# Hybrid decoder block with mixture of experts: down weights in 16 KB rows, column tiles on pairs of activation columns

## The chip, the cores and the metric

The kernel runs on one core of a Trainium2 chip. The metric is device time in microseconds, the median of three executions. A core has TensorE (PE, matmuls, with a weight load called PEld that can overlap them), VectorE (DVE), ScalarE (ACT), GpSimd (POOL) and SyncE (SP). All weights lie in HBM and are brought to SBUF, 128 partitions of on-chip memory, by 16 DMA engines; SP issues nearly all transfers here. TensorE writes its results to PSUM.

## What is computed

One decoder layer: a mixer (an S5 state-space branch beside a convolution branch), then a mixture of 32 experts of which each of 256 tokens takes 4. The mixer ends before the part that this document is about. Of the reference, the experts:

```python
for e in range(N_EXPERTS):                       # 32
    gu = hf @ w_gate_up[e] + b_gate_up[e]        # (256, 1024) @ (1024, 2048)
    g, lin = gu[:, :D_EXPERT], gu[:, D_EXPERT:]
    g = jnp.minimum(g, SWIGLU_LIMIT)
    lin = jnp.clip(lin, -SWIGLU_LIMIT, SWIGLU_LIMIT)
    act = g * jax.nn.sigmoid(SWIGLU_ALPHA * g) * (lin + 1.0)
    out = out + combine[:, e:e + 1] * (act @ w_down[e] + b_down[e])   # (256, 1024) @ (1024, 1024)
```

Everything is fp32. An expert has 8 MiB of gate_up weights and 4 MiB of down weights.

## The kernel before

About the first 230 us belong to the mixer and to the router. Then the experts run in **blocks** of 32 token slots: an expert has at least one block, and more if more than 32 tokens chose it. The number of blocks is read at run time from a plan that VectorE makes; with these inputs there are 46. TensorE runs one block after the other.

**Tiling of a block.** With 32 tokens only 32 columns of the TensorE array would be used, so four matmuls run side by side in four column tiles q = 0 to 3 (`NQ`, `BS` = 32 slots, `QW` = 256 columns). Column tile q works on 256 of the 1024 expert columns and writes PSUM partitions 32q to 32q+31. `bias` (L1450) first writes the gate_up bias into PSUM bank 0, 4 matmuls of 512 columns. `gate_up` (L1461) adds 8 contraction steps k of 4 matmuls; each has 32 tokens as stationary operand (`xT`) and 2 x 256 weight columns as moving operand: 256 for g and 256 for lin, read as two runs of neighbouring words, `row[:, :, QW * q:QW * q + QW]`. An fp32 matmul is two instructions in the trace, so a block's gate_up is 64. `after_gate_up` then scatters the block before, gathers the next tokens (L1418, L1427), transposes the activation in two matmuls (L1489, which read every second column j = 0, 1) and runs `down` (L1474) in two halves h, with `selection` (L1443) and the transpose of the next tokens (L1436) between them.

**Which column is where.** Because L1489 takes every second column, partition p of the transposed activation holds columns 256q + 2p + j. The rows of the down weights must be in the same order: `dn_rows` gives partition p the rows 256q + 2p and 256q + 2p + 1, for the two q of a half. Two rows of 4 KB are 8 KB of neighbouring bytes, and a half has two such runs per partition.

**Loads.** SP issues them in order. Each expert is six DMAs of 2 MiB: four of gate_up (`load_gu`, L365, per partition 16 KB of neighbouring bytes) and two of down (`load_dn`, L368). There are buffers for two experts, `gsl[e % 2]` and `dsl[e % 2]`, so a load for expert e waits until the last block of expert e - 2 has read that buffer (`gu_done`, `dn_done`, with `used_by` from the plan). Of the last expert, the second down half comes in two DMAs (L473, L474). The bias of gate_up comes in four small DMAs (L431) into `bias_rows`, partitions 32q to 32q+31 holding the 32 experts' 2 x 256 columns of tile q.

Of the kernel before, what the change touches and what calls it, by code (L numbers as in the profile page):

```python
# [29 lines left out]
P = 128  # L30
D = 1024
# [12 lines left out]
EXP = 32  # L44
TOPK = 4
BS = 32
NQ = P // BS
QW = D // NQ
# [7 lines left out]
SLOT = 2048  # L56
# [16 lines left out]
def build(nc, T, out):  # L73
    with ExitStack() as ctx:
        def sb(name, shape, dt=F32):
            return ctx.enter_context(nc.sbuf_tensor(name, shape, dt))

        def sem(name):
            return ctx.enter_context(nc.semaphore(name))
# [12 lines left out]
        rC, rD, rE = (ring, C_AT), (ring, D_AT), (ring, E_AT)  # L92
# [3 lines left out]
        rU, rQ = (late, 0), (late, MT * L)  # L96
        rT, rP = (late, 2 * MT * L), (late, 2 * MT * L + 1024)
        rW = sb("rW", [P, 1024])
        base = sb("base", [P, 344 + 3 * 256])
        rX1, rX2, rX3 = (base, 344), (base, 344 + 256), (base, 344 + 512)  # L100

        def view(r, at, *dims, rows=P, dt=F32):
            n = 1
            for d in dims:
                n *= d
            words = n // 2 if dt == BF16 else n
            if isinstance(r, tuple):
                r, at = r[0], r[1] + at
            v = r[0:rows, at:at + words]
            if dt != F32:  # L110
                v = v.bitcast(dt)
            if len(dims) == 2:
                v = v.rearrange("p (a b) -> p a b", b=dims[1])
            if len(dims) == 3:
                v = v.rearrange("p (a b c) -> p a b c", b=dims[1], c=dims[2])
            if len(dims) == 4:
                v = v.rearrange("p (a b c d) -> p a b c d", b=dims[1], c=dims[2], d=dims[3])
            return v
# [49 lines left out]
        rw = view(rF, D, KT, EXP)  # L168
        rb = view(rF, D + 256, EXP)
        hf = [view(rE, 640, D), view(rW, 0, D)]  # L170
        bias_rows = view(rE, 1664, 2 * QW)
        squares = view(rW, 0, D)
        squares2 = view(rC, 2048, 2 * ST, 2, QW)
        scaled = view(ring, KT * SLOT + 2048, ST, NQ, QW)
# [1 line left out]
        xT = view(rX1, 0, 2, NQ, BS)  # L176
# [27 lines left out]
        ebias = view(base, 151, BS)  # L204
# [27 lines left out]
        ps = ctx.enter_context(nc.psum_tensor("ps", [P, 8, 512], F32))  # L232
# [10 lines left out]
        dn_in = [[sem(f"dn_{name}{n}") for n in range(2)] for name in ("even", "odd")]  # L243
# [33 lines left out]
        scales, dn_tail = sem("scales"), sem("dn_tail")  # L277
# [55 lines left out]
        dsl = [[view(ring, DN_AT + odd * DN_ODD + h * 4096, 4096) for h in range(2)] for odd in range(2)]  # L333
# [5 lines left out]

        def dn_rows(e, h):  # L340

            return T["w_down"][0, e].rearrange("(q p j) n -> p q (j n)", q=NQ, j=2)[:, 2 * h:2 * h + 2, :]

        def out_cols(q):

# [5 lines left out]
        def _(sp):  # L351
# [13 lines left out]
                sp.dma_start(gsl[e % 2][n], gu_rows(e, n)).then_inc(gu_in[e % 2][n], 16)  # L365

            def load_dn(e, h):
                sp.dma_start(dsl[e % 2][h].rearrange("p (q c) -> p q c", q=2), dn_rows(e, h)).then_inc(dn_in[e % 2][h], 16)  # L368

            for n in range(2):  # L370
                load(n)
# [12 lines left out]
            for a in range(TG):  # L384
                h = min(SH, TAPS - SH * a)
# [43 lines left out]
            sp.dma_start(gffn, T["norm_ffn_g"][0:1, :].to_broadcast([P, D])).then_inc(late_in, 16)  # L429
            for q in range(NQ):  # L430
                sp.dma_start(bias_rows[BS * q:BS * q + EXP, :].rearrange("e (a c) -> e a c", a=2),  # L431
                             T["b_gate_up"][0].rearrange("e (a n) -> e a n", a=2)[:, :, QW * q:QW * q + QW]
                             ).then_inc(bgu_in, 16)
            used_up(sp, N_IN + 3)
            load_gu(0, 1)
# [18 lines left out]
            def used_by(e):  # L454

                return sp.value_load(blk_last[0:1, e:e + 1], min_val=0, max_val=NBLK - 1)

            for e in range(2, EXP):
                before = used_by(e - 2)
                for n in range(NPAIR):  # L460
                    sp.wait_ge(gu_done, before * KT + PAIR * (n + 1))
                    load_gu(e, n)
                if e < EXP - 1:
                    for h in range(2):
                        sp.wait_ge(dn_done, before * KT + 4 * (h + 1))
                        load_dn(e, h)
                    whole(dn_tail)
                else:
                    sp.wait_ge(dn_done, before * KT + 4)
                    load_dn(e, 0)  # L470
                    sp.wait_ge(dn_done, before * KT + KT)
                    halves = dn_rows(e, 1)
                    sp.dma_start(dsl[e % 2][1][:, 0:SLOT], halves[:, 0, :]).then_inc(dn_in[e % 2][1], 16)  # L473
                    sp.dma_start(dsl[e % 2][1][:, SLOT:], halves[:, 1, :]).then_inc(dn_tail, 16)  # L474
            sp.wait_ge(dn_done, used_by(EXP - 2) * KT + KT)
            sp.dma_start(gfin, T["norm_final_g"].rearrange("(a n) -> a n", a=1).to_broadcast([P, D])
                         ).then_inc(fin_in, 16)
# [684 lines left out]
        def _(pe):  # L1162
# [3 lines left out]
            for c, rows, at in ((2, META, 0), (0, P, META), (1, P, META + P)):  # L1166
                pe.wait_ge(x_in[c], 16)
                for k in range(KT):
                    if c == 2 and k == KT - 1:
                        pe.wait_ge(gmix_cols, 1)  # L1170
                    ins = nc.tensor.transpose(ps[:, k, at:at + rows], xin[0:rows, c, k * P:(k + 1) * P],
                                              ident[0:rows, 0:rows])
# [159 lines left out]
            for n in range(KT):  # L1332
# [5 lines left out]
                for g in range(2):  # L1338
# [4 lines left out]
                    for k in range(MT):  # L1343
                        ins = nc.tensor.matmul(ps[:, bank(use), g * S:(g + 1) * S], w[:, k, (n % 4) * P:(n % 4) * P + P],  # L1344
                                               ya[:, k, :], start=(k == 0), stop=(k == MT - 1))
# [7 lines left out]
            for n in range(KT):  # L1353
# [5 lines left out]
                for k in range(MT):  # L1359
                    ins = nc.tensor.matmul(ps[:, bank(use), 0:S], w[:, k, (n % 4) * P:(n % 4) * P + P], cacc[:, k, :],  # L1360
                                           start=(k == 0), stop=(k == MT - 1))
# [23 lines left out]
            for c in range(ST):  # L1385
                for k in range(KT):
# [7 lines left out]
                    for h in range(2):  # L1394
                        ins = nc.tensor.matmul(ps[:, 4 + 2 * c + h, :], merged[:, k, c * P:(c + 1) * P],  # L1395
                                               w[:, k % 2, 512 * h:512 * h + 512], start=(k == 0), stop=(k == KT - 1))
# [50 lines left out]
            def bias():  # L1447

                for q in range(NQ):
                    nc.tensor.matmul(ps[BS * q:BS * q + BS, 0, :], ebias[BS * q:BS * q + EXP, :],  # L1450
                                     bias_rows[BS * q:BS * q + EXP, :], start=True, stop=False, skip_group_check=True,
                                     tile_position=(BS * q, BS * q))

            def gate_up(e, odd, first, until):
                for k in range(PAIR * first, PAIR * until):
                    n = k // PAIR
                    if k % PAIR == 0:
                        pe.wait_ge(gu_in[odd][n], e * 8 + 16 - 8 * odd)
                    row = gsl[odd][n][:, (k % PAIR) * SLOT:(k % PAIR) * SLOT + SLOT].rearrange("p (a c) -> p a c", a=2)
                    for q in range(NQ):  # L1460
                        ins = nc.tensor.matmul(ps[BS * q:BS * q + BS, 0, :].rearrange("p (a c) -> p a c", a=2),  # L1461
                                               xT[:, k % 2, k // 2, :], row[:, :, QW * q:QW * q + QW],
                                               start=False, stop=(k == KT - 1), skip_group_check=True,
                                               tile_position=(0, BS * q))
                    ins.then_inc(gu_done, 1)
# [53 lines left out]
            for c in range(ST):  # L1519
                ins = nc.tensor.matmul(ps[0:EXP, 1, 96:97], maskb[:, c, :], onesb[:, 0:1], start=(c == 0), stop=(c == 1))  # L1520
# [56 lines left out]
```

## Time and profile before

| | us |
|---|---|
| median of 3 executions | 1186.16 |
| lowest and highest | 1185.9, 1186.97 |
| the profiled execution | 1185.86 |
| its span in the trace | 1184.1 |
| TensorE busy in it | 982.7 (83%) |
| VectorE, ScalarE, GpSimd busy | 305.9, 143.0, 14.9 |

The page counts 69355 DMA packets with 435.39 MB. Of the chain that ended last, 43% of the span is TensorE and 41% DMA. How to read it: a busy TensorE is not one at its peak; a share over the whole span mixes stretches with different limits, so the stretches have to be looked at one by one. In a row of the trace the part behind "<-" is what was read, or what was waited for.

### The profile page before, as it was taken

Reading aid. Unit: us, or ns where it says so; the run is one execution under the profiler, and the core shown is the slowest. Engines: PE = TensorE matmul, PEld = TensorE weight load, DVE = VectorE, ACT = ScalarE, POOL = GpSimd, SP = SyncE. Lnnn points to the kernel's source line nnn. Section 1 sums busy time; section 2 is a strip of 40 time slices with the busy share of each in tenths; the row PEclk is TensorE's granted clock in tenths of the full one; section 3 lists DMA queues with packets and bytes.
Section 4 is the critical chain, followed back from the end, with each engine's and each line's share of the span. In section 5 each row is a group of like instructions: output and inputs, shape, how many; then the busy total and the mean of one; then the engine's idle time right before and its main releaser. Section 6 shows DMA issues by size and latency. Waiting matters only on the chain.

```text
span 1184.1 us, 23761 instructions
## 1 busy us (share of the span) xinstructions
PE 982.7 (83%) x10042; PEld 457.3 (39%) x10043; DVE 305.9 (26%) x908; ACT 143.0 (12%) x335; POOL 14.9 (1%) x26
## 2 busy tenths in 40 slices
PE   8999999979986666659999987689766898876685
PEld 6887886423332222223333332233222333322232
DVE  5999842511110000001111111011100111110012
ACT  2311230301110000001111110011000100100012
POOL 1111000000000000000000000000000000000000
PEclk9999999989998788899999999899988999998898
DMA  9772786791999999998899999999999999999994
GB/s 260 225 181 95 261 337 249 296 415 50 431 426 426 426 426 427 427 426 366 341 390 401 426 426 425 425 426 428 426 425 426 426 426 426 426 426 426 426 427 183
DMA packets 69355, 435.39 MB, mean 368 GB/s; under 512 B 15104, under 2 KB 31424, under 8 KB 36560
## 3 DMA queue, kind: packets, MB, share of 16 engines
q1 hardware_dynamic: 69184, 434.93, 89.7%
q8 instruction: 18, 0.29, 0.1%
q10 hardware_dynamic: 144, 0.09, 0.0%
q14 instruction: 9, 0.07, 0.0%
HBM read 432.21 MB, written 1.05 MB: 366 GB/s over the span
## 4 chain that ended last, share of the span: by engine, by line
PE 43%; DMA 41%; DVE 9%; SPq 3%; issue 2%; ACT 1%; ACTq 0%; DVEq 0%
DMA ring<-in_w_down 20%; PE ps L1461 16%; DMA ring<-in_w_gate_up 16%; PE ps L1474 8%; DMA early<-in_w_gate_up 4%; PE ps L1450 2%; PE ps L1344 2%; PE ps L1395 2%; PE ps L1206 2%; SPq L368 2%; PE ps L1427 2%; PE ps L1418 2%; SPq L365 1%; PE ps L1360 1%; PE ps L1443 1%
## 5 line engine op out<-in xcount | busy, mean ns | idle before, releaser
L1461 PE MATMUL ps<-ring,base 128*32 128x512 f32 x2208 | 283.3, 655 | 81.0 <-DMA ring<-in_w_gate_up 80.9
L1474 PE MATMUL ps<-ring,base 128*32 128x256 f32 x2944 | 177.9, 382 | 41.0 <-DMA ring<-in_w_down 22.6
L1461 PEld LDWEIGHTS ps<-ring,base 128*32 128x32 f32 x2208 | 67.3, 115 | 290.0 <-issue 162.4
L1474 PEld LDWEIGHTS ps<-ring,base 128*32 128x32 f32 x2944 | 90.2, 110 | 100.3 <-ACT base L693 31.4
L1123 DVE TENSOR_SCALAR base<-ps 128x256 f32<-128x256 f32 x46 | 19.5, 425 | 390.1 <-PE ps L1461 390.1
L1206 PE MATMUL ps<-ring 128*128 128x256 f32 (+1 forms) x448 | 102.5, 387 | 0.0
L1130 DVE COPY base<-ps 128x256 f32<-128x256 f32 x46 | 19.5, 425 | 312.3 <-PE ps L1474 312.3
L691 ACT ACTIVATE base<-base 128x256 f32<-128x256 f32 x46 | 19.2, 416 | 661.9 <-DVE base L1123 661.9
L1206 PEld LDWEIGHTS ps<-ring 128*128 128x128 f32 x448 | 84.4, 191 | 15.1 <-issue 1.4
L1450 PE MATMUL ps<-ring,base 32*32 32x512 f32 x368 | 51.4, 628 | 24.1 <-issue 23.6
L1461 PE MATMUL ps<-early,base 128*32 128x512 f32 x368 | 50.6, 673 | 17.8 <-DMA early<-in_w_gate_up 17.7
L1461 PE MATMUL ps<-late,base 128*32 128x512 f32 x368 | 47.0, 630 | 16.5 <-DMA late<-in_w_gate_up 16.5
L1427 PE MATMUL ps<-base,late 32*128 32x256 f32 x752 | 58.1, 426 | 2.2 <-issue 2.2
L1427 PEld LDWEIGHTS ps<-base,late 32*128 32x128 f32 x752 | 36.8, 201 | 51.0 <-issue 49.2
L1108 DVE TENSOR_SCALAR early<-base 128x32 f32<-128x32 f32 x92 | 23.4, 298 | 39.1 <-issue 36.5
L1461 PEld LDWEIGHTS ps<-early,base 128*32 128x32 f32 x368 | 11.7, 117 | 52.2 <-DMA early<-in_w_gate_up 27.2
L1418 PE MATMUL ps<-ring,early 128*32 128x256 f32 x376 | 30.2, 392 | 1.1 <-DVE early L1064 1.1
L1461 PEld LDWEIGHTS ps<-late,base 128*32 128x32 f32 x368 | 11.4, 112 | 48.3 <-DMA late<-in_w_gate_up 24.2
L1443 PE MATMUL ps<-base,early 128*32 128x128 f32 x736 | 29.6, 279 | 0.0
L677 ACT COPY base<-ps 128x256 f32<-128x256 f32 x47 | 17.5, 372 | 100.0 <-PE ps L1436 100.0
L1418 PE MATMUL ps<-rW,early 128*32 128x256 f32 x376 | 28.9, 379 | 0.0
L1344 PE MATMUL ps<-late,ring 128*128 128x256 f32 x128 | 28.2, 380 | 0.5 <-issue 0.5
(328 smaller groups left out, 682.7 us busy)
## 6 DMA issues: line engine op xcount, KB each, us to landing
ring<-in_w_gate_up SPq DMA_DIRECT2D x96, 2048.0 KB, 38.1
ring<-in_w_down SPq DMA_DIRECT2D x63, 2048.0 KB, 40.6
late<-in_w_gate_up SPq DMA_DIRECT2D x16, 2048.0 KB, 40.5
early<-in_w_gate_up SPq DMA_DIRECT2D x16, 2048.0 KB, 39.8
ring<-in_w_in SPq DMA_DIRECT2D x14, 1024.0 KB, 7.8
ring<-in_w_out SPq DMA_DIRECT2D x4, 1024.0 KB, 12.5
ring<-in_w_s_lin SPq DMA_DIRECT2D x2, 1024.0 KB, 6.3
ring<-in_w_s_gate SPq DMA_DIRECT2D x2, 1024.0 KB, 5.1
```

What stands on the lines that cost most here:

```text
L368: sp.dma_start(dsl[e % 2][h].rearrange("p (q c) -> p q c", q=2), dn_rows(e, h)).then_inc(dn_in[e % 2][h], 16)
L1108: ins = nc.vector.tensor_scalar(wsel[:, c, :], slots, cur[:, c:c + 1], cur[:, 2 + c:3 + c], ALU.is_equal, ALU.mult)
L1123: nc.vector.tensor_scalar(act_in, g_out, LIMIT, None, ALU.min).then_inc(g1_ready, 1)
L1206: ins = nc.tensor.matmul(ps[:, z % 2, 0:L - n0], w[:, k, (z % 2) * P:(z % 2) * P + P], h[:, k, n0:L], start=(k == 0), stop=(k == KT - 1))
L1344: ins = nc.tensor.matmul(ps[:, bank(use), g * S:(g + 1) * S], w[:, k, (n % 4) * P:(n % 4) * P + P], ya[:, k, :], start=(k == 0), stop=(k = ...
L1395: ins = nc.tensor.matmul(ps[:, 4 + 2 * c + h, :], merged[:, k, c * P:(c + 1) * P], w[:, k % 2, 512 * h:512 * h + 512], start=(k == 0), sto ...
L1418: ins = nc.tensor.matmul(ps[BS * q:BS * q + BS, 2, 0:QW], onehot[:, c, :], hf[c][:, QW * q:QW * q + QW], start=(c == 0), stop=(c == ST - 1 ...
L1427: ins = nc.tensor.matmul(ps[:, 4 + q, QW * c:QW * c + QW], selT[BS * q:BS * q + BS, c * P:(c + 1) * P], ysb[BS * q:BS * q + BS, :], start= ...
L1443: ins = nc.tensor.matmul(ps[BS * q:BS * q + BS, 3, S + c * P:S + (c + 1) * P], of[:, c, :], ident[:, :], start=True, stop=True, tile_posit ...
L1450: nc.tensor.matmul(ps[BS * q:BS * q + BS, 0, :], ebias[BS * q:BS * q + EXP, :], bias_rows[BS * q:BS * q + EXP, :], start=True, stop=False, ...
L1461: ins = nc.tensor.matmul(ps[BS * q:BS * q + BS, 0, :].rearrange("p (a c) -> p a c", a=2), xT[:, k % 2, k // 2, :], row[:, :, QW * q:QW * q ...
L1474: ins = nc.tensor.matmul(ps[BS * q:BS * q + BS, 1, 0:QW], actT[:, n % 2, n // 2, :], row[:, out_cols(q)], start=(n == 0), stop=(n == KT - ...
```

## The change

Partition p of the down weights now gets four neighbouring rows 4p to 4p+3 of a half (512 rows), which are 16 KB of neighbouring bytes, in one run. So the transposed activation must hold, in partition p, columns 512h + 4p + j' with j' = 0 to 3. The transposes stay as they were (every second column of a column tile), so column tile q now works on the columns 512(q // 2) + 4n + 2(q % 2) + (0, 1): pairs, at every fourth. `gate_up` reads its moving operand in that pattern out of the same weight rows, and writes PSUM in the same order of addresses as before. `bias` reads its operand in the same pattern (`act_cols`); for this each group of 32 partitions of `bias_rows` holds 2 x 512 columns in place of 2 x 256, loaded by the same four DMAs, now of 128 KB each, into a new region at the end of `base` (8 KB more per partition). To make room, the scratch for software DMAs is set to 1024 bytes.

```diff
@@ the region for the bias @@
-        base = sb("base", [P, 344 + 3 * 256])
+        base = sb("base", [P, 344 + 3 * 256 + 2 * D])
...
-        bias_rows = view(rE, 1664, 2 * QW)
+        bias_rows = view(base, 344 + 3 * 256, 2 * 2 * QW)
@@ the down weights' rows, and the columns of tile q @@
         def dn_rows(e, h):
-            return T["w_down"][0, e].rearrange("(q p j) n -> p q (j n)", q=NQ, j=2)[:, 2 * h:2 * h + 2, :]
+            return T["w_down"][0, e].rearrange("(h p j) n -> p h (j n)", h=2, j=4)[:, h, :]
+
+        def act_cols(row, q):
+            return row.rearrange("p (a n j) -> p a n j", a=2, j=4)[:, :, :, 2 * (q % 2):2 * (q % 2) + 2]
@@ loads @@
             def load_dn(e, h):
-                sp.dma_start(dsl[e % 2][h].rearrange("p (q c) -> p q c", q=2), dn_rows(e, h)).then_inc(dn_in[e % 2][h], 16)
+                sp.dma_start(dsl[e % 2][h], dn_rows(e, h)).then_inc(dn_in[e % 2][h], 16)
...
                 sp.dma_start(bias_rows[BS * q:BS * q + EXP, :].rearrange("e (a c) -> e a c", a=2),
-                             T["b_gate_up"][0].rearrange("e (a n) -> e a n", a=2)[:, :, QW * q:QW * q + QW]
+                             T["b_gate_up"][0].rearrange("e (a h n) -> e a h n", a=2, h=2)[:, :, q // 2, :]
                              ).then_inc(bgu_in, 16)
...
-                    sp.dma_start(dsl[e % 2][1][:, 0:SLOT], halves[:, 0, :]).then_inc(dn_in[e % 2][1], 16)
-                    sp.dma_start(dsl[e % 2][1][:, SLOT:], halves[:, 1, :]).then_inc(dn_tail, 16)
+                    sp.dma_start(dsl[e % 2][1][:, 0:SLOT], halves[:, 0:SLOT]).then_inc(dn_in[e % 2][1], 16)
+                    sp.dma_start(dsl[e % 2][1][:, SLOT:], halves[:, SLOT:]).then_inc(dn_tail, 16)
@@ TensorE @@
             def bias():
                 for q in range(NQ):
-                    nc.tensor.matmul(ps[BS * q:BS * q + BS, 0, :], ebias[BS * q:BS * q + EXP, :],
-                                     bias_rows[BS * q:BS * q + EXP, :], start=True, stop=False, skip_group_check=True,
+                    nc.tensor.matmul(ps[BS * q:BS * q + BS, 0, :].rearrange("p (a n j) -> p a n j", a=2, j=2),
+                                     ebias[BS * q:BS * q + EXP, :], act_cols(bias_rows[BS * q:BS * q + EXP, :], q), start=True, stop=False, skip_group_check=True,
                                      tile_position=(BS * q, BS * q))
...
                     for q in range(NQ):
-                        ins = nc.tensor.matmul(ps[BS * q:BS * q + BS, 0, :].rearrange("p (a c) -> p a c", a=2),
-                                               xT[:, k % 2, k // 2, :], row[:, :, QW * q:QW * q + QW],
+                        half = row[:, :, 2 * QW * (q // 2):2 * QW * (q // 2) + 2 * QW]
+                        ins = nc.tensor.matmul(ps[BS * q:BS * q + BS, 0, :].rearrange("p (a n j) -> p a n j", a=2, j=2),
+                                               xT[:, k % 2, k // 2, :], half.rearrange("p a (n j) -> p a n j", j=4)[
+                                                   :, :, :, 2 * (q % 2):2 * (q % 2) + 2],
                                                start=False, stop=(k == KT - 1), skip_group_check=True,
                                                tile_position=(0, BS * q))
...
-    nc = bacc.Bacc("TRN2", target_bir_lowering=False, num_devices=1)
+    nc = bacc.Bacc("TRN2", target_bir_lowering=False, num_devices=1, dynamic_dma_scratch_size=1024)
```

No instruction is added, taken away or moved on any engine; only operands change.

## Rows read from the trace of the kernel before

**Rows 1.** The page, 40 equal slices of the span: GB/s moved by the DMA engines.
```profile
GB/s 260 225 181 95 261 337 249 296 415 50 431 426 426 426 426 427 427 426 366 341 390 401 426 426 425 425 426 428 426 425 426 426 426 426 426 426 426 426 427 183
```

**Rows 2.** Windows: length, busy us of PE, PEld, DVE, ACT, POOL, PEclk, DMA share, GB/s.
```profile
324.00:530.00 206.00, 140.64 (x1440) 47.70 (x1432) 21.67 (x80) 14.46 (x40) 0.00 (x0) 0.88 1.01 426
560.00:656.00 96.00, 91.46 (x1144) 36.88 (x1140) 17.56 (x66) 10.85 (x30) 0.00 (x0) 1.00 0.88 369
656.00:1136.00 480.00, 383.75 (x4358) 143.05 (x4350) 67.30 (x253) 42.23 (x117) 0.00 (x0) 0.94 1.01 426
```

**Rows 3.** The chain in order of time: start us, us, what; three pieces of it.
```profile
253.87 1.93 PE ps L1450 x8
...
328.17 1.68 SPq L365
...
530.22 1.93 PE ps L1474 x32
...
533.41 7.00 PE ps L1461 x64
...
548.20 1.06 PE ps L1450 x8
549.26 7.00 PE ps L1461 x64
...
659.48 32.41 DMA ring<-in_w_down
...
1093.68 42.44 DMA ring<-in_w_down
```

**Rows 4.** L1461 on PE, whole span: duration ns min/median/max, first and last start us.
```profile
L1461 PE MATMUL ps<-ring,base x2208: 592/592/1062, 231.6 to 1159.0; 128*32 128x512 f32 x184
L1461 PE MATMUL ps<-late,base x368: 592/592/1061, 261.1 to 1160.7; 128*32 128x512 f32 x184
```

**Rows 5.** Windows with only w_down packets, only gate_up packets, and the same again.
```profile
373.00:380.00 7.00, 6.53 (x74) 2.62 (x70) 1.19 (x3) 1.06 (x3) 0.00 (x0) 0.81 1.02 424
384.00:398.00 14.00, 7.23 (x52) 1.48 (x52) 1.74 (x8) 0.00 (x0) 0.00 (x0) 0.81 1.01 428
402.50:409.50 7.00, 6.53 (x62) 2.61 (x58) 1.19 (x3) 1.06 (x3) 0.00 (x0) 0.73 1.02 424
413.50:427.50 14.00, 7.79 (x52) 1.54 (x52) 1.74 (x8) 0.00 (x0) 0.00 (x0) 0.85 1.01 428
```

**Rows 6.** DMA, three windows: 372:381 (w_down), 383:399 (gate_up), 371.9:401.4 (packets alone).
```profile
DMA packets 480, 3.80 MB, mean 422 GB/s; under 512 B 16, under 2 KB 16, under 8 KB 16
q1 hardware_dynamic: 480, 3.80, 101.3%
...
DMA packets 466, 6.85 MB, mean 428 GB/s; under 512 B 48, under 2 KB 48, under 8 KB 48
q1 hardware_dynamic: 466, 6.85, 100.5%
...
DMA packets 1119, 12.58 MB, mean 426 GB/s; under 512 B 96, under 2 KB 96, under 8 KB 96
```

**Rows 7.** SP's queue in order of time: start us, us, what.
```profile
291.33 2.06 SPq L365 DMA_DIRECT2D ring<-in_w_gate_up  x2
```

**Rows 8.** PEld at two lines: L1489 reads every second word, L1436 neighbouring words.
```profile
L1489 PEld LDWEIGHTS ps<-base x92: 194/208/221, 241.2 to 1165.2; 128*128 128x128 f32 x92
L1436 PEld LDWEIGHTS ps<-base x94: 137/140/143, 230.4 to 1168.0; 128*128 128x128 f32 x94
```

**Rows 9.** PEld in order of time: two loads of each of those lines.
```profile
298.43 0.31 PEld L1489 LDWEIGHTS ps<-base 128*128 128x128 f32 x2 [0.41 <-issue]
...
301.27 0.20 PEld L1436 LDWEIGHTS ps<-base 128*128 128x128 f32 x2 [0.41 <-issue]
```

**Rows 10.** SP's queue in order of time, at the bias loads.
```profile
165.90 2.54 SPq L431 DMA_DIRECT2D ring<-in_b_gate_up  x4
173.68 0.34 SPq L365 DMA_DIRECT2D ring<-in_w_gate_up  x1
```

## What I expect of the time

> **What bounds the kernel now.** Read the slices first. From the eleventh slice (296 us) on the DMA engines move about 426 GB/s in nearly every slice, with a dip between 530 and 650 us [rows 1]. The stretches say it sharper: 426 GB/s from 324 to 530 us, 369 GB/s from 560 to 656 us while TensorE is busy 91.46 of 96 us, then 426 GB/s up to 1136 us [rows 2]. The chain of waits changes hands in the same places [rows 3]. It is TensorE's from 253.87 to 328.17 us, the transfers' until a piece of `w_down` releases TensorE at 530.22, TensorE's until 659.48, the transfers' until `w_down` lands at 1136.12, and TensorE's from there to the end. So there are two kinds of stretch. Where an expert has one block of 32 tokens, streaming its 12 MiB of weights takes longer than its matmuls; where experts with several blocks follow each other, TensorE is late. The chain holds 5 blocks in the first TensorE stretch, 8 in the second, 2 in the last: 15 gate_up groups of 7.00 us [rows 3]. Over the span there are 2208 + 368 gate_up matmuls [rows 4] and 368 more whose weights lie in `early`: 2944, or 64 in each of 46 blocks.
>
> **Term 1: down weights in 16 KB rows.** Per DMA of 2 MiB the change halves the packets: 256 of 8 KB become 128 of 16 KB; over 16 engines that is 16 against 8 for each. The rows of the profile show both sizes, since gate_up already moves 16 KB rows. Windows that hold only `w_down` run at 424 and 424 GB/s, windows that hold only gate_up at 428 and 428 [rows 5]. 2.097 MB at 424 is 4.946 us, at 428 it is 4.900: 0.046 us saved per DMA, the low bound. The packets themselves give the high bound [rows 6]. In the 9 us of 8 KB rows, 464 packets (480 less 16 small ones) took 101.3% of 16 engines: 16 x 9 x 1.013 / 464 = 314 ns each. In the 16 us of 16 KB rows, 418 packets took 100.5%: 615.5 ns each. Two of the small ones are 13.3 ns longer than one large one; 8 such pairs are 0.106 us per DMA. I take 0.075, the middle, because window edges cut packets in the first and busy time overlaps a little (over 100%) in the second.
>
> How many such DMAs lie on the path? Only those served while the queue is never empty and the landing releases TensorE. From 291.33 us, when the fourth expert's weights are first asked for [rows 7], to the landing at 530.22 are 239 us; one expert takes 29.5 us (12.58 MB in that window) [rows 6], so 8.1 experts or 16 down DMAs. In the TensorE stretch until 656 us the saving is not worth anything: DMA has idle time there. From 656.8 to 1136.1 us are 16.2 experts or 32 DMAs. Sum 48 x 0.075 = 3.6 us, with bounds 48 x 0.046 = 2.2 and 48 x 0.106 = 5.1. The last expert's second half is still cut into two DMAs of 8 KB rows, and it lands after the piece at 1136 that sets the end: nothing. The first three experts' down weights load before 291 us, where no piece of the chain is a transfer (its one gap is 7.12 us of "issue", a wait for nothing that the profile shows): nothing.
>
> Here a rule of the Trainium skill is worth weighing. [rows 6] show 13.3 ns for an extra packet and the rates in [rows 5] 0.046 us over 8 packets, or 5.8 ns. The Trainium skill (DMA: Bandwidth & Descriptors, "Why small descriptors are slow (HBM only)") states a fixed cost of about 3 cycles per packet inside the DMA engine and calls joining descriptors worthwhile only up to 256 B; at the 850 MHz that page gives, 3.5 ns x 8 x 48 is an estimate of 1.4 us in place of 3.6, or 1184.8.
>
> **Term 2: gate_up reads its moving operand in pairs.** The count of matmuls, their shapes and the order stay. Each still streams 512 columns, but now 2 of every 4 neighbouring fp32 words, while another column tile reads the other 2. This cost is not in the trace: no matmul before reads its moving operand with a step. Bounds from rows: at the low end nothing (not below: the same columns are streamed and no instruction is saved). At the high end stands the only strided read of TensorE, the weight load of the activation's transpose (every second word): 208 ns against 140 for the same load of neighbouring words [rows 8], a factor 1.49. Which is nearer? Look at what that strided load delivers. Two of them fill 0.31 to 0.32 us, of which one is 0.208, so the second begins about 0.11 us after the first: 128 columns in 0.11 us, 0.86 ns each. Two contiguous ones fill 0.20 us, 0.06 us apart: 0.47 ns each [rows 9]. A gate_up group needs less than that contiguous rate: 64 matmuls, four side by side, in 7.00 us are 437 ns for 512 columns, 0.85 ns each. One strided stream with two useful words in 16 bytes thus delivers just what an fp32 matmul takes, and pairs also keep 8 bytes together. I take zero. What speaks against it is that four column tiles read at once, and four strided streams at once are not in the trace.
>
> The Trainium skill (Advanced Engine Details and Errata, "SBUF Cachelines") says that at least two hits in a 16-byte line give full performance. Pairs have two, so by that rule term 2 is zero and the sum stays. The weight load in [rows 8] also has two hits and is slower than the contiguous one: here the row does not agree, so I don't let the rule carry the zero.
>
> The `bias` matmuls read pairs too; 8 of them in 1.06 us, in every block [rows 3]; same reasoning, zero, or half of it at the factor 1.49. What covers a slower gate_up: only the one-block experts in the DMA stretches (TensorE is busy 140.64 of 206 us there [rows 2]). In the 15 blocks on the chain there is no cover.
>
> **Term 3: the rest.** The four bias loads double from 64 to 128 KB and are issued at 165.90 us [rows 10]. That is 0.25 MiB more, 0.6 us at 428 GB/s, and they wait for nobody's buffer: the next load on the same queue is issued 5 us later, at 173.68. They now land in a region of their own. Taken as zero; 0.6 us if the cover were gone. The smaller scratch for software DMAs touches no transfer of this kernel: all sit in queues of SP and ACT. PSUM is written in the same order as before, so nothing changes for VectorE and ScalarE; and the transposes read as before.
>
> **The sum** against the profiled run: 1185.86 measured, of which the span is 1184.1, so 1182.3 there. That run is 0.3 us under the median, so against 1186.16: 1186.16 - 3.6 = **1182.5 us**.
>
> **Rivals.** *A, the packets cost less than they seem, or other waits absorb it.* The rates are the only direct comparison and their low bound gives 2.2 us or less: 1184.0 to 1186.2. For it: 424 and 428 differ by 1%, near what such a window can resolve. Against it: two pairs of windows agree, and packet times point the same way. The estimate from the Trainium skill above, 1184.8, falls in this case.
>
> *B, four strided streams starve TensorE.* Place: gate_up and bias, 7.00 + 1.06 = 8.06 us per block. It decides from a slow-down of 3%: 15 blocks x 8.06 = 121 us, and 3.6/121 = 3%. At factor 1.49 a block gets 4 us longer. About 3.5 blocks lie before DMA restarts at 291 us (14 us), 8 in the middle (32), 2 at the end (8); less 3.6: 1186.2 + 50 = about 1236. At factor 2 a block would take 15.9 + 8.1 = 24 us (15.9 is from one start of gate_up to the next [rows 3]); two-block experts are then all slower than their weights, and TensorE's own floor decides: 253.9 + 45 x 24 + 12 after the last block = 1346. For it: the factor in [rows 8], and the doubling of the stored bytes that each stream walks over. Against it: the rate in [rows 9] suffices, and gate_up's matmuls take 592 ns as minimum and as median over the whole span, while DMA, VectorE and ScalarE use the same memory beside them [rows 4]: nothing there looks near a limit.
>
> *C, the change doesn't do what it says:* if the hardware cut 16 KB rows for `w_down` otherwise than for gate_up, the packets stay. Against it: gate_up's 128 x 4096 words give 16 KB packets [rows 6]. It ends as A.
>
> **Chances.** Forecast 0.60 (1181 to 1184), A and C 0.16 (1184 to 1187), B 0.24, of which mild (3 to 10%, up to 1195) 0.06, near 1.5 times 0.10, near 2 times 0.08. The range is 1180.5 to 1191: it takes in the forecast's bounds, A, and the mild end of B; the heavy B of 0.18 is left out. About 0.2% (2.4 us) is what a measurement of this kernel can tell from no change, so the line is at 1183.8: of the forecast's 0.60, 0.04 falls inside. Faster 0.56, same 0.21, slower 0.23.
>
> **What the profile after would show.** Right: `w_down` packets of 16 KB, some 8,000 packets fewer in all; about 428 GB/s in stretches that had 426; gate_up at 7.0 us for 64 matmuls, 592 ns median; `w_down` released TensorE about 1.2 us earlier at 530 and 3.6 us earlier at 1136. A: packets halved, rate at 426. B: gate_up groups over 7.2 us, and DMA idle in more slices. Wrong altogether: the 592 ns median moves, or the landing at 530 does not.

## The result, and the profile after

| | before | after |
|---|---|---|
| median of 20 runs each, us | 1185.38 | 1187.74 |
| lowest and highest, us | 1184.41, 1186.97 | 1185.64, 1188.79 |
| profiled execution, us | 1185.86 | 1186.65 |
| its span, us | 1184.1 | 1184.9 |

The changed kernel takes 1.0019 times the time of before, 95% interval 1.0012 to 1.0026: 2.4 us more, just inside the 0.2% that the prediction set as its line. The forecast was 1182.5. The time is within the range of 1180.5 to 1191, but it moved to the other side: 5.2 us above the forecast. The profiled execution of after lies 1.1 us under its median and that of before 0.5 us above its own, so the two traces differ by only 0.8 us of span.

The page of after: GB/s in 40 slices, and the packets of the whole run.
```profile
GB/s 257 228 189 89 269 346 239 307 408 45 432 427 430 428 429 429 427 429 349 345 381 382 430 428 428 429 426 431 427 429 426 429 428 428 429 428 429 427 428 163
DMA packets 61291, 435.65 MB, mean 368 GB/s; under 512 B 15104, under 2 KB 31168, under 8 KB 36560
```
The windows of after (columns as in [rows 2]).
```profile
324.00:530.00 206.00, 141.16 (x1468) 47.23 (x1464) 21.66 (x81) 14.46 (x40) 0.00 (x0) 0.91 1.01 428
560.00:656.00 96.00, 91.96 (x1110) 35.61 (x1106) 17.46 (x66) 10.20 (x28) 0.00 (x0) 1.00 0.86 361
656.00:1136.00 480.00, 388.34 (x4404) 142.54 (x4396) 67.34 (x254) 42.99 (x119) 0.00 (x0) 0.95 1.01 428
```
The transfers do what was foretold: 428 GB/s where [rows 1, 2] have 426. Only in the middle do they move less, 361 against 369. That is the stretch in which TensorE is late: a load there waits until a slower block has read its buffer.

Now gate_up and `bias` on PE over the whole span (duration ns min/median/max, first and last start).
```profile
L1466 PE MATMUL ps<-ring,base x2208: 608/613/1063, 231.2 to 1158.9; 128*32 128x512 f32 x184
L1454 PE MATMUL ps<-base x368: 603/622/1055, 228.8 to 1155.1; 32*32 32x512 f32 x184
```
[rows 4] had 592 as minimum and median. Now the minimum is 608: no matmul of this form is as fast as the commonest one before. The chain of after in order of time:
```profile
529.20 1.94 PE ps L1480 x32
...
531.33 1.10 PE ps L1454 x8
532.43 7.45 PE ps L1466 x57
...
548.81 7.45 PE ps L1466 x58
...
662.26 31.36 DMA ring<-in_w_down
...
1135.43 1.93 PE ps L1480 x32
```
Against [rows 3]: the gate_up of a block takes up to 7.45 us, not 7.00. The `x57` means that some records are missing; the 64 matmuls are all run. `bias` takes 1.10 us against 1.06. The chain gives a ledger. The first gate_up of the middle TensorE stretch starts at 532.43 (533.41 before): 1.0 us gained. That stretch ends at 662.26 (659.48): now 2.8 us lost, so it cost 3.8: 0.47 in each of its 8 blocks. The last wait for the weights ends at 1135.43 (1136.17 before, the row below): 0.7 us gained, so the transfers gave back 3.5. After that come two blocks with 0.9 us more, and 0.7 us in the last scatter (1.90 us for its 16 matmuls against 1.18). Around that scatter, from 1172.8 to 1174.8 us, the mean granted clock was 0.61 in that execution and 0.88 in the one of before: that part is of these two executions. Sum: -1.0 + 3.8 - 3.5 + 0.9 + 0.7 = +0.9, and the spans differ by 0.8.
```profile
1136.17 1.93 PE ps L1474 x32
```

So both halves of the change are in plain sight, and each is about as large as the other. What has to be found out is whether each half does that alone, and why a read in pairs is slower.

### The profile page after: what moved, and what is told of

The parts are those of the page before. It is cut to its first block, busy times and chain, and to the rows that moved or that the text cites. A ratio compares the mean times of both kernels' runs of the same rounds, so it can differ in the third digit from the quotient of the medians.

```text
span 1184.9 us, 23761 instructions
## 1 busy us (share of the span) xinstructions
PE 989.7 (84%) x10042; PEld 454.2 (38%) x10043; DVE 305.7 (26%) x908; ACT 143.0 (12%) x335; POOL 14.9 (1%) x26
## 2 busy tenths in 40 slices
DMA packets 61291, 435.65 MB, mean 368 GB/s; under 512 B 15104, under 2 KB 31168, under 8 KB 36560
## 4 chain that ended last, share of the span: by engine, by line
PE 47%; DMA 37%; DVE 9%; SPq 3%; issue 2%; ACT 1%; another core or an unknown queue 0%; ACTq 0%; DVEq 0%
DMA ring<-in_w_gate_up 24%; PE ps L1466 18%; PE ps L1480 8%; DMA early<-in_w_gate_up 7%; DMA ring<-in_w_down 6%; SPq L369 3%; PE ps L1431 3%; PE ps L1454 2%; PE ps L1348 2%; PE ps L1399 2%; PE ps L1422 2%; PE ps L1210 2%; PE ps L1447 1%; PE ps L1364 1%; PE ps L1495 1%
## 5 line engine op out<-in xcount | busy, mean ns | idle before, releaser
L1466 PE MATMUL ps<-ring,base 128*32 128x512 f32 x2208 | 289.8, 665 | 79.5 <-DMA ring<-in_w_gate_up 79.4
L1466 PEld LDWEIGHTS ps<-ring,base 128*32 128x32 f32 x2208 | 66.2, 113 | 294.1 <-issue 171.1
L1480 PEld LDWEIGHTS ps<-ring,base 128*32 128x32 f32 x2944 | 88.7, 110 | 99.9 <-ACT base L697 30.6
L1454 PE MATMUL ps<-base 32*32 32x512 f32 x368 | 51.4, 627 | 24.0 <-issue 23.8
L1466 PE MATMUL ps<-late,base 128*32 128x512 f32 x368 | 50.5, 669 | 15.8 <-DMA late<-in_w_gate_up 15.8
```

The lines of the kernel that those rows point to most:

```text
L1480: ins = nc.tensor.matmul(ps[BS * q:BS * q + BS, 1, 0:QW], actT[:, n % 2, n // 2, :], row[:, out_cols(q)], start=(n == 0), stop=(n == KT - ...
```

## The experiments

Medians of before, from the same chip each time: 1185.26 us (9 runs) beside the first four, 1184.96 (13) beside the next four, 1185.41 (27) beside the last three. e3 to e7 ran once each, the others five times or more. In e1 to e7 the columns and the rows of the down weights don't match, so they compute another sum of the experts; the work is the same. Code lines are shortened, and `...` stands for what is left out.

### Each half alone

**e1**, 16 KB rows for the down weights alone:
```
-  return T["w_down"][0, e].rearrange("(q p j) n -> p q (j n)", q=NQ, j=2)[:, 2 * h:2 * h + 2, :]
+  return T["w_down"][0, e].rearrange("(h p j) n -> p h (j n)", h=2, j=4)[:, h, :]
```


> The kernel before with the down weights' part of the change alone: 16 KB rows per partition; gate_up and bias read neighbouring words as before. The activation's columns then don't match the order of the down rows, so the experts' sum is a different one; the work is the same. Theory S (the change has two effects that add: transfers 3.6 us better, strided gate_up about 0.45 us per block worse on 15 blocks of the chain): 3.6 us under the kernel before (2.5 to 5), w_down windows at 428 GB/s, gate_up matmuls at 592 ns. Rival W (16 KB writes of w_down disturb TensorE's reads, and that is what made gate_up slower): gate_up matmuls at about 613 ns here too, and the time within 1 us of the change's.

**e2**, the pairs of gate_up alone (`bias` and the down weights as before):
```
-  matmul(ps[BS*q:BS*q+BS, 0, :].rearrange("p (a c) -> p a c", a=2), xT[:, k % 2, k // 2, :],
-         row[:, :, QW * q:QW * q + QW], ...)
+  half = row[:, :, 2 * QW * (q // 2):2 * QW * (q // 2) + 2 * QW]
+  matmul(ps[BS*q:BS*q+BS, 0, :].rearrange("p (a n j) -> p a n j", a=2, j=2), xT[:, k % 2, k // 2, :],
+         half.rearrange("p a (n j) -> p a n j", j=4)[:, :, :, 2 * (q % 2):2 * (q % 2) + 2], ...)
```


> The kernel before with the gate_up part of the change alone: column tiles read pairs at every fourth; bias and down weights as before (columns and down rows then don't match, the work is the same). Theory S: gate_up matmuls at 613 ns, a block's group at 7.45 us in place of 7.00, the time 5 to 7 us above the kernel before. Rival W: matmuls at 592 ns and no difference in time.

e1 took 1181.21 us, ratio 0.9966 (0.9952 to 0.9979): 4.05 us faster. e2 took 1190.33, ratio 1.0039 (1.0026 to 1.0053): 5.1 us slower. Together +1.0; the whole change measured +2.4, within what two intervals of 1.6 us each allow, and `bias` in pairs (0.04 us per block) is in neither. Windows, chain and restart of e1:
```profile
324.00:530.00 206.00, 138.04 (x1464) 47.69 (x1456) 21.80 (x81) 14.46 (x40) 0.00 (x0) 0.90 1.01 428
...
228.88 1.07 PE ps L1418 x16
...
256.07 7.59 PE ps L1461 x64
...
290.37 2.04 SPq L365 DMA_DIRECT2D ring<-in_w_gate_up  x2
...
531.11 7.00 PE ps L1461 x64
...
657.25 32.19 DMA ring<-in_w_down
...
1131.20 1.93 PE ps L1474 x32
```
gate_up, chain and restart of e2:
```profile
L1462 PE MATMUL ps<-ring,base x2208: 609/613/1063, 232.2 to 1163.9; 128*32 128x512 f32 x184
...
228.92 1.07 PE ps L1418 x16
...
293.17 2.17 SPq L365 DMA_DIRECT2D ring<-in_w_gate_up  x2
...
535.40 7.45 PE ps L1462 x58
...
664.58 31.58 DMA ring<-in_w_down
...
1140.44 1.93 PE ps L1476 x32
```
The restart of after, then two rows of before's chain that the readings below use:
```profile
291.68 2.13 SPq L369 DMA_DIRECT2D ring<-in_w_gate_up  x2
```
```profile
228.35 1.07 PE ps L1418 x16
...
255.80 8.87 PE ps L1461 x64
```
The same points of the chain in all four kernels, in us (the restart is where SP first issues the fourth expert's weights, [rows 7] for before; the columns of e1, e2 and after are differences to before, summed up to that point):

| | before | e1 | e2 | after |
|---|---|---|---|---|
| restart of the transfers | 291.33 | -0.96 | +1.84 | +0.35 |
| first gate_up of the middle stretch | 533.41 | -2.30 | +1.99 | -0.98 |
| end of that stretch | 659.48 | -2.23 | +5.10 | +2.78 |
| last wait for the weights ends | 1136.17 | -4.97 | +4.27 | -0.74 |

Read e1 from row to row. Between restart and middle stretch it gains 1.34 us, in the middle nothing, in the second long stretch 2.74. That is the prediction's account of 16 and 32 DMAs: 0.084 and 0.086 us each, where 0.075 was taken. The 0.96 us at the restart are not from the rows: the first block's L1418 starts 0.53 us later than before's, and then one gate_up group takes 7.59 us where before has 8.87, at a mean granted clock of 0.87 against 0.77 (254 to 266 us).

e2 reads the other way. It is 1.84 us late at the restart; 0.57 of that it already is at the first block's L1418 (228.92 against 228.35), so the three blocks and a quarter in between cost 1.27. It pays next to nothing while the transfers set the pace (+0.15), 3.11 us in the middle (8 blocks of 0.39), and 0.85 in the last two blocks. From the middle to the last wait it gets 0.83 back. After shows the same beside e1: 3.52 us gained there against 2.74. The rows show where this comes from: the `w_down` transfer that the end of the middle stretch releases takes 32.41 us to land in before and 31.58 in e2, 32.19 in e1 and 31.36 in after. Presumably a later TensorE finds a shorter queue there; that is read off these rows, and no run varies it by itself. The half that costs and the half that gains lie in different stretches, so neither hides the other.

### Why is a read in pairs slower?

It could be the number of 16-byte lines that the stream walks over (two words used of each four), the breaks in the run of addresses, or four streams competing with each other, in pairs for the same lines.

**e3**, runs of four words at every eighth; **e4**, single words at every second (`half` as in e2).
```
e3: half.rearrange("p a (n j) -> p a n j", j=8)[:, :, :, 4 * (q % 2):4 * (q % 2) + 4]
e4: half.rearrange("p a (n j) -> p a n j", j=2)[:, :, :, 1 * (q % 2):1 * (q % 2) + 1]
```


> The kernel before, gate_up reading runs of four words at every eighth (whole lines of 16 bytes), bias and down as before; the columns don't match the down rows. If the cost of a strided stream hangs on how many 16-byte lines it touches (L): matmuls back at 592 ns and groups at 7.00 us, since whole lines are used. If it hangs on the breaks in the address (R, one per run): half as many breaks as pairs, so about 602 ns and 7.2 us.

> The kernel before, gate_up reading every second word, so that two column tiles share each line and each still uses two words of every 16-byte line, as with pairs; the columns don't match the down rows. L (lines touched): 613 ns and 7.45 us as with pairs. R (breaks in the address): twice the breaks of pairs, so about 634 ns and 7.9 us or more.

gate_up in e3 and, below the dots, in e4:
```profile
L1462 PE MATMUL ps<-ring,base x2208: 592/592/1062, 231.5 to 1157.7; 128*32 128x512 f32 x184
...
L1462 PE MATMUL ps<-ring,base x2208: 609/612/1062, 231.6 to 1162.8; 128*32 128x512 f32 x184
```
e3, whose stream also jumps (128 times in 512 words), is as fast as neighbouring words: 592 ns, 7.00 us for a group, 1184.48 us in one execution. e4 jumps after each word, twice as often as pairs do, and costs the same as pairs: 612 ns, 1189.9 us. So neither the breaks nor the length of the stretch that is walked over are it; what counts is how many useful words lie in four neighbouring ones.

**e5**, pairs in column tile 0 alone (`if q == 0`), the other three with neighbouring words; **e6**, all four in pairs, but the odd tiles from the buffer's other slot, so that no two tiles read the same line:
```
e6: at = ((k + q) % PAIR) * SLOT
    part = gsl[odd][n][:, at:at + SLOT].rearrange("p (a c) -> p a c", a=2)
    ... half.rearrange("p a (n j) -> p a n j", j=4)[:, :, :, 0:0 + 2]
```


> The kernel before with pairs read by column tile 0 alone; tiles 1 to 3 read neighbouring words (tile 0's columns then are others than the down rows expect). Theory C (the four streams compete for lines, so each strided stream adds its part): matmuls between 592 and 613 ns, a group near 7.1 us, the time about 1 to 1.5 us above the kernel before. Theory O (one strided stream is slower by itself and the group of four waits for its slowest): a group near 7.4 us as with all four, and tile 0's matmuls longer than the others'.

> The kernel before with pairs in all four tiles, but no two tiles in the same lines: the odd tiles read pairs at the same offset from the neighbouring weight row (columns and rows then don't match the reference). If two tiles that walk through the same lines get in each other's way: matmuls back near 592 ns and 7.00 us. If only the number of lines per stream counts (C or O): 613 ns and 7.4 us as with pairs.

e5 first: the strided tile, the three others, and its chain over one block and the start of the next; then e6.
```profile
L1463 PE MATMUL ps<-ring,base x552: 609/648/1062, 231.5 to 1166.7; 128*32 128x512 f32 x184
L1469 PE MATMUL ps<-ring,base x1656: 592/592/1062, 231.5 to 1166.3; 128*32 128x512 f32 x184
...
533.80 1.06 PE ps L1450 x8
...
542.68 1.08 PE ps L1427 x16
...
550.51 1.06 PE ps L1450 x8
```
```profile
L1464 PE MATMUL ps<-ring,base x2208: 609/612/1062, 231.8 to 1162.9; 128*32 128x512 f32 x184
```
In e6 nothing changes against pairs that share their lines (612 ns, 1190.0 us). In e5 the three tiles with neighbouring words keep their 592 ns and the strided one is slow with no other strided one beside it: competition between strided streams, or for the same lines, is not what makes a strided stream slow. That it would be as slow alone on the array, no run shows. And e5 took 1194.8 us, 9.8 above before, and neither theory had that: one strided tile of four costs more than four. Its gate_up lasts from 534.86 to 542.68, 7.8 us and not 7.45, and from one block's start to the next are 16.7 us where [rows 3] have 15.85. The weight loads, one in front of each matmul, show the rhythm. In e5, two neighbouring rounds of the three others (`x3`) and of tile 0 (`x1`):
```profile
602.68 0.12 PEld L1469 LDWEIGHTS ps<-ring,base 128*32 128x32 f32 x3 [0.26 <-issue]
602.80 0.11 PEld L1463 LDWEIGHTS ps<-ring,base 128*32 128x32 f32 x1
603.12 0.12 PEld L1469 LDWEIGHTS ps<-ring,base 128*32 128x32 f32 x3 [0.21 <-issue]
603.28 0.11 PEld L1463 LDWEIGHTS ps<-ring,base 128*32 128x32 f32 x1
```
On the mean of a longer stretch the three run ahead at 0.43 us a round and tile 0 follows at 0.49; now and then the others wait for it (0.56 us from one of their rounds, at 606.12 us, to the next). So the tiles are out of step, and tile 0 is slower than the 0.45 us of four strided ones. Why a strided stream is slower beside neighbours that are not, stays open.

**e7**, one useful word in each four (`[:, :, :, q:q + 1]`, all tiles over the same 1024 words):

> The kernel before with gate_up reading one word of every four: tile q reads words 4n + q, one word per 16-byte line (columns don't match the down rows). If a stream gets one line in the time of two words, as the weight load's 0.86 ns per word at two per line suggests, one word per line doubles the stream: about 850 ns for 512 columns, matmuls near 1040 ns, a group near 14 us, the time near 1350 us. If each line costs only a small extra over the 427 ns of neighbouring words (pairs: 128 lines more, about 27 ns more): 384 lines more, about 80 ns, a group near 8.3 us, the time near 1200 us.

```profile
L1462 PE MATMUL ps<-ring,base x2208: 1059/1079/1147, 231.6 to 1322.0; 128*32 128x512 f32 x184
...
555.83 14.62 PE ps L1462 x62
```
It took 1352.99 us. Now there are three points for one constant. A gate_up group is 16 rounds of four matmuls side by side. The time of a round is the step from one group of four weight loads to the next: two of before (13 rounds apart), two of after (six apart), two of e7 (two apart).
```profile
305.39 0.13 PEld L1461 LDWEIGHTS ps<-ring,base 128*32 128x32 f32 x4 [0.30 <-issue]
...
310.96 0.13 PEld L1461 LDWEIGHTS ps<-ring,base 128*32 128x32 f32 x4 [0.30 <-issue]
```
```profile
601.24 0.13 PEld L1466 LDWEIGHTS ps<-late,base 128*32 128x32 f32 x4 [0.34 <-issue]
...
603.96 0.14 PEld L1466 LDWEIGHTS ps<-early,base 128*32 128x32 f32 x4 [0.33 <-issue]
```
```profile
603.62 0.15 PEld L1462 LDWEIGHTS ps<-ring,base 128*32 128x32 f32 x4 [0.73 <-issue]
...
605.42 0.15 PEld L1462 LDWEIGHTS ps<-ring,base 128*32 128x32 f32 x4 [0.75 <-issue]
```
A round of e7 takes 900 ns for 512 lines of four words: 1.76 ns per line. A round of pairs takes 453 ns for 256 lines: 1.77 ns. With quads or neighbouring words a round has 128 lines, some 225 ns by that rate, and the round takes 428 because the words themselves need that (0.84 ns each). With all four tiles alike, a stream takes the longer of the two: 0.84 ns per word or 1.77 ns per line. At two words per line the lines are the longer by some 6%: 0.4 us in the 16 rounds, which is what a block of e2 pays.

The Trainium skill (Advanced Engine Details and Errata, "SBUF Cachelines") asks for at least two hits on a 16-byte line to absorb the access latency. These runs agree that four neighbouring words are the unit, that one hit costs (14.62 us a group) and that four are free. At two hits they differ: some 6% of a round (453 against 428 ns) are not absorbed, in e4 and e6 too (612 ns, as with pairs).

### Can the gain be had without the cost?

Partition p of a down half must hold four neighbouring rows to have 16 KB; so its transposed activation must hold columns 4p to 4p + 3. The change got that from gate_up. Two other places could give it.

**e8**, longer rows on the other tensor: gate_up loaded in DMAs of 4 MiB with 32 KB per partition where the buffer allows. A load now starts only when the second of its two buffers is free, and TensorE waits for both; the rest is as before.

> The kernel before, with gate_up's weights loaded in DMAs of 4 MiB with 32 KB per partition wherever two buffers lie side by side (both pairs of an even expert, the first of an odd one, from the third expert on); a buffer is asked for when the second of the two is free, and TensorE waits for both. If what a packet costs beyond its bytes is fixed (9.4 ns, from 0.075 us per DMA with 8 packets fewer per engine): 0.075 us per such DMA, 3 per two experts, some 36 on the chain's saturated stretches, 2.7 us under the kernel before. If 32 KB rows are cut back to 16 KB packets: no gain, or up to 1 us slower by the coarser waits.

Its page, its last window, and its waits (engine line waited for: us in total, times, longest us), with those of before last:
```profile
DMA packets 62875, 435.39 MB, mean 367 GB/s; under 512 B 14384, under 2 KB 30704, under 8 KB 35840
...
656.00:1136.00 480.00, 382.29 (x4336) 147.16 (x4332) 67.20 (x253) 41.57 (x115) 0.00 (x0) 0.92 1.01 428
...
PE ps L1475 <- DMA ring<-in_w_gate_up: 102.8, 23, 6.9
```
```profile
PE ps L1461 <- DMA ring<-in_w_gate_up: 80.9, 39, 4.2
```
The rate is there, 428 GB/s, with 69355 - 62875 = 6480 packets fewer. The time is 1188.69 us, ratio 1.0028 (1.0018 to 1.0038): 3.7 us slower, where 2.7 us less was expected. A matmul that waits for a landing now finds the piece twice as large: the longest wait is 6.9 us where before has 4.2, the total 102.8 where it has 80.9. Twice the matmuls stand behind each landing, and the path pays for that at the end of an expert. At the end of the last stretch that the transfers bound, the last piece of gate_up releases TensorE at nearly the same time in both traces, 1126.94 us in e8 and 1126.23 in before. But e8 then still has 32 matmuls (5.34 us) of it to do and before 16 (3.40), and the next block's gate_up starts at 1141.40 against 1139.63. What the coarser asking for buffers adds is not taken apart. Here, longer rows on a larger DMA lost more than they gained.

**e9**, the kernel before, with the activation stored by VectorE in the order in which the transposes read it, so that the strided weight load of [rows 8] goes:
```
-  nc.vector.tensor_scalar(act_in, g_out, LIMIT, None, ALU.min)
+  nc.vector.tensor_scalar(act_in.rearrange("p (j n) -> p j n", j=2), g_out.rearrange("p (n j) -> p j n", j=2), ...)
...
-  transpose(..., act_in.rearrange("p (n j) -> p j n", j=2)[:, j, :], ...)
+  transpose(..., act_in[:, j * P:(j + 1) * P], ...)
```


> The kernel before with the activation stored in the order of the transposes: VectorE reads PSUM at every second column and writes neighbouring words, so the transposes' weight loads (L1489) read neighbouring words. All results are those of the reference. Theory K (a stream gets one 16-byte line in about 1.76 ns, whichever it is): the weight load falls from 208 to 140 ns, the pair of transposes by some 0.1 us, in about 11 blocks that count 1 us under the kernel before. Rival V (VectorE's read of PSUM at every second column costs as much): its two instructions rise above 425 ns and nothing is gained.

**e10**, 16 KB down rows with gate_up and `bias` on neighbouring words; the activation is turned by 8 small matmuls of 64 columns against the identity, with VectorE storing every fourth column together, and `down` reading the turned copy in that order (both left out here):
```
+  for j in range(4):
+      for o in range(2):
+          matmul(ps[64*o:64*o+64, 3, 64*j:64*j+64].rearrange("p (h s) -> p h s", h=2), act_in[:, 64*j:64*j+64],
+                 ident.rearrange("p (h o s) -> p h o s", h=2, o=2)[:, :, o, :], ...)
```


> Down weights in 16 KB rows with gate_up and bias reading neighbouring words: the transposes are cut into 8 matmuls (4 columns of every four, for even and odd column tiles on the lower and upper 64 partitions), with the activation stored in that order by VectorE. All results are those of the reference. The gain of the transfers (4.05 us with that part alone) stays if the step from the activation to its transposed copy grows by less than 0.37 us in each of about 11 blocks that count. Expected 0.2 us more per block: 1.5 to 2.5 us under the kernel before. If eight small matmuls take 0.5 us more per block: 1 to 2 us above it.

**e11**, the changed kernel with the stored order of e9.

> The changed kernel with the activation stored in the order of the transposes, as in the kernel e9_act_order. All results are those of the reference. By theory K 1 us under the changed kernel, that is about 1.3 us above the kernel before; by rival V equal to the changed kernel.

The weight loads of the turned activation in e9 and VectorE's instruction there, then e10's matmuls for the turning in one block, and before's.
```profile
L1491 PEld LDWEIGHTS ps<-base x92: 137/140/143, 240.7 to 1163.5; 128*128 128x128 f32 x92
L1123 DVE TENSOR_SCALAR base<-ps x46: 424/425/426, 238.7 to 1161.5; 128x256 f32<-128x256 f32 x46
```
```profile
605.62 0.69 PE L1492 MATMUL ps<-base 128*64 128x64 f32 x16
```
```profile
606.19 0.50 PE L1489 MATMUL ps<-base 128*128 128x128 f32 x2
```
e9: 1184.31 us, ratio 0.9993 (0.9984 to 1.0002). The load is down from 208 to 140 ns, the pair of transposes on the chain from 0.45 to 0.38 us, and VectorE pays nothing for the other order (424/425/426 ns at L1123, whole span, with both). 0.07 us in the 13 blocks that pay is 0.9 us, and 1.1 was measured, though the interval takes in no change. e11: 1186.32, ratio 1.0007 (0.9998 to 1.0017), 1.4 us under the changed kernel's 1187.74. That fits the same step, though the two medians are from different chips and no interval was taken between them. e10: 1184.24, ratio 0.9992 (0.9983 to 1.0001), 1.2 us faster where at least 1.5 was expected, and its interval too takes in no change. It has the transfers' gain (428 GB/s in both long stretches), and 0.19 us more in each block: 0.69 against 0.50 for the turning, in some 13 paying blocks 2.5 us of the 4.

So of the ways tried to get the down rows to 16 KB, none keeps the 4 us of e1. The best is e10, and no run settles that it beats the kernel before.

## Why the prediction was wrong, point by point

**Term 1, the rows of 16 KB: right.** Forecast 3.6 us (2.2 to 5.1), measured 4.05 (2.5 to 5.7) in e1, and the places are right too: 1.3 us by the middle stretch (foretold 1.2), 2.7 in the second long stretch (foretold 2.4, the difference of 3.6 and 1.2). After has 3.5 there, of which 0.8 is what e2 gets back there too, without the rows. The remark that the down weights of the first three experts load before 291 us and gain nothing holds as far as the traces tell: the 0.96 us by which e1 restarts earlier are less than what one gate_up group gains by its granted clock. Rival A falls, its price of 2.2 us or less is under e1's interval. With it falls the estimate of 1.4 us from the fixed cost per packet that the Trainium skill states (DMA: Bandwidth & Descriptors, "Why small descriptors are slow (HBM only)"): 4.05 us over 48 DMAs of 8 packet pairs is 10.5 ns per extra packet, and that page's figure gave 3.5. Rival C falls: 69355 packets became 61291, 8064 fewer for the 8,000 foretold.

**Term 2, the pairs: the step that failed.** It says: "One strided stream with two useful words in 16 bytes thus delivers just what an fp32 matmul takes ... I take zero." It was built on 0.86 ns per word delivered and 0.85 needed. Both numbers had two digits, and the first was a difference of 0.31 and 0.208 us, rounded by more than the gap between them. From such an equality nothing follows on which side one is. Delivered are 453 / 512 = 0.88 ns per word, and needed are 0.84: about 0.4 us per group in place of zero. The prediction itself had the break-even at 3% of gate_up and `bias`, 8.06 us. What after pays per block, 0.47 us, is 6% of that and enough to turn the sign; such an equality should have been given even odds of that.

The count of 15 blocks was off too, in both directions. Of the first TensorE stretch only what lies before the restart at 291 us pays, since from there to 530 the transfers set the pace; and one more block pays, the one before 253.87 us. That makes 3.25 blocks, then 8, then 2: 13 in place of 15. Nor does each of them take 7.00 us as the prediction read: the first of its 15 takes 8.87, at the lower granted clock. e2, without `bias`, should have 13 x 0.39 = 5.1 us by this; of those 0.8 comes back behind the middle stretch, and its median lies 5.1 above before, with 1.6 either way.

**Rival B, four strided streams starve TensorE: its mild end is what happened, by another mechanism.** It had 3 to 10% and up to 1195, with a chance of 0.06. The time fits, the name doesn't: e5 and e6 show a stream to be slow whether or not the others are strided or share its lines. The heavy cases (1.49 and 2 times) took the weight load's duration as the measure, but two loads of 208 ns fill only 0.31 us [rows 9], so part of each overlaps the other. It is the spacing of loads that carries over: 64 lines in about 0.11 us are 1.7 ns per line, near the 1.77 of gate_up.

The `bias` matmuls, which the prediction also took at zero, go from 587 and 603 ns (minimum and median, the row below) to 603 and 622, 0.04 us per block.
```profile
L1450 PE MATMUL ps<-ring,base x368: 587/603/1057, 229.4 to 1155.5; 32*32 32x512 f32 x184
```

**Term 3: right.** Nothing of the larger bias loads shows in the ledger.

**The signs named ahead:** 428 GB/s and 8,000 packets came as foretold; the "wrong altogether" sign, a median other than 592 ns, came too. Rival B's "gate_up groups over 7.2 us" came with 7.45. TensorE was released 1.0 us earlier at 530 (1.2 foretold), but at 1136 only 0.7 and not 3.6: the middle stretch had used up the gain.

## What to carry to other kernels

Where the bound changes hands between transfers and an engine, price each edit in its own stretches: a gain in one and a cost in the other do not hide each other, they add. A rate that comes out just high enough from two rounded rows doesn't say yet on which side it lies. Read it as a coin toss, and set against it the break-even, or measure it with one matmul form at 1, 2 and 4 useful words per line, as e7, e2 and e3 do.

## What the runs showed of the hardware that was not expected

- A moving fp32 operand of 512 columns in four column tiles that all read alike costs the longer of 0.84 ns per word and 1.77 ns per group of four neighbouring words touched: rounds of 428 ns (four useful words of four, with or without jumps between the fours), 453 (two), 900 (one).
- One strided column tile beside three with neighbouring words is slower than four strided ones: 648 against 613 ns, 7.8 against 7.45 us for a group, 1194.8 us (once) against 1190.3. The tiles fall out of step; the cause is open.
- VectorE wrote the activation in a permuted order, reading PSUM at every second fp32, in the same 425 ns.
- DMAs of 2 MiB gain about 0.085 us each when their rows go from 8 to 16 KB; 4 MiB with 32 KB rows ran at the same 428 GB/s as 16 KB rows.
